# First four x tiles of a hybrid encoder step loaded as rows and turned by TensorE, before and after

## The reference, cut to what matters

```python
seq = concatenate([meta_tokens, x], axis=1)
cq, ckv_raw, kpe_raw, mq, mk, mv, mo, mi, mf, za, zb = project(rmsnorm(seq, norm_gain), w_in)   # h @ w_in
# attention from cq, ckv, kpe; mLSTM from mq, mk, mv, mo, mi, mf; gates za, zb
y = x_res + concatenate([a, m], axis=-1) @ w_out
```

## Time and profile before

| | us |
|---|---|
| median of 3 runs | 1995.39 (1994.79 to 1996.48) |
| the profiled execution | 1995.78 |
| its span, first to last instruction | 1994.0 |
| TensorE busy | 1985.5 |
| VectorE busy | 1254.3 |
| ScalarE busy | 911.5 |
| mean granted TensorE clock | 0.999 |

### The profile page before, as it was taken

One profiled execution on the slowest core, in us unless ns is written; L12 is line 12 of the kernel. 1 busy time (PEld: TensorE's weight loads), 2 busy tenths in 40 slices (PEclk: granted clock), 3 DMA queues, 4 the chain that ended last, 5 costly groups with the idle time before them and its releaser, 6 DMA issues.

```text
span 1994.0 us, 36219 instructions
## 1 busy us (share of the span) xinstructions
PE 1985.5 (100%) x14762; PEld 1961.7 (98%) x14762; DVE 1254.3 (63%) x2474; ACT 911.5 (46%) x1810; POOL 192.7 (10%) x228
## 2 busy tenths in 40 slices
PE   9999999999999999999999999999999999999998
PEld 9999999999999999999999999999999999999998
DVE  7856677677576786868777555444455664444444
ACT  5564456565444443434444444444444553333333
POOL 0011143433200000000000001000000000000000
PEclk9999999999999999999999999999999999999999
DMA  9765443333455554645545655565556556666665
GB/s 249 197 187 157 113 120 117 99 111 119 122 170 147 149 169 128 179 127 175 157 145 170 169 169 168 168 170 168 173 169 171 169 183 193 193 193 193 193 193 142
DMA packets 219262, 323.24 MB, mean 162 GB/s; under 512 B 28240, under 2 KB 100264, under 8 KB 219096
## 3 DMA queue, kind: packets, MB, share of 16 engines
q1 hardware_dynamic: 215800, 317.71, 55.3%
q10 hardware_dynamic: 3296, 3.22, 0.5%
HBM read 310.06 MB, written 9.62 MB: 160 GB/s over the span
## 4 chain that ended last, share of the span: by engine, by line
PE 99%; DVE 0%; DMA 0%; ACTq 0%; ACT 0%; issue 0%
PE bank L1884 31%; PE bank L1887 30%; PE bank L1888 30%; PE bank L2150 1%; PE bank L2120 1%; PE bank L2046 1%; PE bank L2049 1%; PE bank L2048 1%; PE bank L2222 0%; PE bank L2248 0%; PE bank L2116 0%; PE bank L2117 0%; DMA xt<-in_meta_tokens_dram 0%; PE bank L2260 0%; PE bank L2064 0%; PE bank L2065 0%
## 5 line engine op out<-in xcount | busy, mean ns | idle before, releaser
L1215 DVE TENSOR_TENSOR wlo<-raw,whi 128x512 fp32r<-128x512 f32 (+1 forms) x1256 | 811.0, 655 | 681.5 <-ACT whi L801 671.5
L1884 PE MATMUL bank<-xsplit,whi 128*128 128x288 f32 (+2 forms) x4128 | 1217.2, 295 | 2.4 <-DVE xsplit L1239 2.1
L1888 PE MATMUL bank<-xsplit,wlo 128*128 128x288 f32 (+2 forms) x4128 | 1212.1, 294 | 0.0
L1887 PE MATMUL bank<-xsplit,whi 128*128 128x288 f32 (+2 forms) x4128 | 1211.9, 294 | 0.0
L801 ACT CAST whi<-raw 128x512 fp32r<-128x512 f32 (+1 forms) x1256 | 706.8, 576 | 954.9 <-PE bank L1888 911.6
L1884 PEld LDWEIGHTS bank<-xsplit,whi 128*128 128x128 f32 (+1 forms) x4128 | 773.2, 187 | 5.1 <-issue 3.4
L1887 PEld LDWEIGHTS bank<-xsplit,whi 128*128 128x128 f32 (+1 forms) x4128 | 773.2, 187 | 2.0 <-issue 1.0
L1888 PEld LDWEIGHTS bank<-xsplit,wlo 128*128 128x128 f32 (+1 forms) x4128 | 772.8, 187 | 0.0
L1884 PE MATMUL bank<-latents,whi 128*128 128x288 f32 (+1 forms) x352 | 112.7, 320 | 0.2
L1887 PE MATMUL bank<-latents,whi 128*128 128x288 f32 (+1 forms) x352 | 106.9, 304 | 0.0
L1888 PE MATMUL bank<-latents,wlo 128*128 128x288 f32 (+1 forms) x352 | 106.7, 303 | 0.0
(11 more groups left out here) (301 smaller groups left out, 1254.8 us busy)
## 6 DMA issues: line engine op xcount, KB each, us to landing
raw<-in_w_in_dram SPq DMA_DIRECT2D x313, 512.0 KB, 3.8
raw<-in_w_out_dram SPq DMA_DIRECT2D x128, 512.0 KB, 3.8
raw<-in_w_in_dram SPq DMA_DIRECT2D x142, 256.0 KB, 3.1
raw<-in_w_q_up_dram SPq DMA_DIRECT2D x48, 384.0 KB, 3.3
raw<-in_w_kv_up_dram SPq DMA_DIRECT2D x16, 512.0 KB, 3.7
xres<-in_x_prompt_dram SPq DMA_DIRECT2D x32, 128.0 KB, 3.7
xt<-in_x_prompt_dram SPq DMA_DIRECT2D x28, 128.0 KB, 4.9
out_dram<-ytok SPq DMA_DIRECT2D x28, 128.0 KB, 3.5
```

The lines of the kernel that those rows point to most:

```text
L1215: ins = tt(lo, src, hi.bitcast(f32), ALU.subtract)
L1884: ins = mm(out, w_hi, m_hi, start=start, stop=False, **kw)
L1887: mm(out, w_hi, m_lo, start=False, stop=False, **kw)
L1888: return mm(out, w_lo, m_hi, start=False, stop=stop, **kw)
```

## The change

The first four tiles of x (512 features) are loaded with tokens in rows into a new buffer xp (96 partitions, four pieces of tokens: 96, 96, 96 and the 16 meta rows) and turned by TensorE, four transposes a tile, into banks 4 to 7. ScalarE and VectorE read them from the bank instead of from xs. To leave these banks free, the order of the first eight units is changed: k = 0 to 3 of columns 0 to 511 first (banks 0 to 3), then k = 0 to 3 of columns 512 to 1023; from unit 8 on it is as before. Tiles 0 and 1 are turned before the first matmul, tile 2 behind unit 0, tile 3 behind unit 1. The first 256 features of x are waited for before the transposes of tiles 0 and 1, the second 256 before that of tile 2. The fillers are 11, and after the transposes of tiles 0 and 1 there are eight transposes of the identity. All chunks have four tiles; chunk 0 keeps its features in natural order. xt still gets chunk 0, for the row sums, now by SP ahead of the weights of k = 13. The waits of SP's meta transfers and of ScalarE's queue for the memset are gone.

```diff
-CHUNKS = [(0, 2), (2, 2)] + [(k, 4) for k in range(4, KT, 4)]
+CHUNKS = [(k, 4) for k in range(0, KT, 4)]
+X_LED = 4
+X_TOK = [(N_META, 96), (N_META + 96, 96), (N_META + 192, 96), (0, N_META)]
-X_AHEAD = 2
-HALVES = 3
-WARM = 16
-X_PIECES = [12 if b in (0, 2, 3) else 4 for b in range(len(CHUNKS))]
-NAR_LOADS = [6, 4, 4, 4]
+HALVES = 2
+WARM = (11, 8)
+X_PIECES = [16, 12, 12] + [4] * (len(CHUNKS) - 3)
+NAR_LOADS = [4, 4, 4, 4]
...
+        def led_rows(eng, block, tiles):
+            a, z = 2 * P * block, 2 * P * block + 2 * P
+            rows, got = (x_prompt[0, 0:192, a:z], xp_in if block else x_in[0])
+            if tiles == 2:
+                eng.dma_start(xp[:, 0:2, a:z], rows.rearrange("(t p) c -> p t c", p=96)).then_inc(got, 16)
+            else:
+                eng.dma_start(xp[0:64, 2, a:z], x_prompt[0, 192:256, a:z]).then_inc(got, 16)
+        def part_of(u):
+            return (u % X_LED, u // X_LED) if u < 2 * X_LED else (u // 2, u % 2)
+        def x_after(u):
+            if u < X_LED:
+                return u
+            k = (u + 1) // 2
+            return k if u % 2 and X_LED <= k < KT else None
...
+            first_weights(0, (0,))
+            led_rows(sp, 0, 2)
+            first_weights(0, (1,))
+            led_rows(sp, 1, 2)
+            led_rows(sp, 1, 1)
+            for n in range(1, X_LED):
+                first_weights(n)
+            x_rows(sp, 1)
+            sp.wait_ge(eps_set, 4)
+            ends(1, 1)
+            first_weights(4)
+            ends(2, len(CHUNKS) - 2)
+            for k in range(5, KT):
                 if k % 4 == 3 and k < KT - 1:
                     x_rows(sp, chunk_of(k + 1))
+                if k == 13:
+                    x_rows(sp, 0)
+                    ends(0, 1)
                 first_weights(k)
...
-            x_end_rows(act, 0, 2, x_sample[0], range(4))
-            act.wait_ge(eps_set, 2)
-            x_end_rows(act, 0, 2, meta, (2, 3))
+            led_rows(act, 0, 1)
+            act.dma_start(xp[0:N_META, 3, :], meta[:, 0:X_LED * P]).then_inc(x_in[0], 16)
+            act.dma_start(xp[64:96, 2, :], x_sample[0, :, 0:X_LED * P]).then_inc(x_in[0], 16)
...
+            for u in range(2 * KT + AHEAD):            # ScalarE; VectorE in the same order
+                if u < 2 * KT:
+                    two_units(u)
+                    if x_after(u) is not None:
+                        x_tile(x_after(u))
...
+            for _ in range(WARM[0]):
                 mm(bank[3][:, 0:P], rB[:, 0:P], rB[:, 0:P], start=True, stop=True)
             pe.wait_ge(ident_in, 16)
+            def x_tile(k):
+                fill("x", 4 + k)
+                for t, (c0, n) in enumerate(X_TOK):
+                    ins = tr(bank[4 + k][:, c0:c0 + n], xp[0:n, t, k * P:k * P + P], ident[0:n, 0:n])
+                ins.then_inc(full[4 + k], 1)
+            pe.wait_ge(x_in[0], 16 * 4)
+            for k in range(2):
+                x_tile(k)
+            for _ in range(WARM[1]):
+                tr(bank[3][:, 0:P], ident, ident)
+            for u in range(2 * KT):
+                k, half = part_of(u)
+                pe.wait_ge(lo_done, u + 1)
+                if k < X_LED:
+                    pe.wait_ge(free[4 + k], use("x", 4 + k) + 1)
+                else:
+                    pe.wait_ge(xlo_d, k - X_LED + 1)
...
+                if u < 2:
+                    if u == 0:
+                        pe.wait_ge(xp_in, 16 * 2)
+                    x_tile(u + 2)
```

More of the change, by code:

```diff
@@ L96 @@
 PHASES = [
+    ("x", 1, (0, 0, 0, 0, 1, 1, 1, 1)),
     ("cq_two", 1, (1, 1, 1, 1, 1, 1, 1, 1)),
@@ L201, in gain_columns @@
     for k, m in CHUNKS:
-        t[:, G_X + k:G_X + k + m] = rows[k * P:(k + m) * P].reshape(P, m)
+        block = rows[k * P:(k + m) * P]
+        t[:, G_X + k:G_X + k + m] = block.reshape(P, m) if k else block.reshape(m, P).T
     for at, name in ((G_QR, "q_rope_norm"), (G_KR, "k_rope_norm")):
@@ L459, in w_rows @@
             k0, m = CHUNKS[chunk_of(k)]
-            return w_in[k0 * P:(k0 + m) * P, cols].rearrange("(p k) c -> p k c", k=m)[:, k - k0:k - k0 + n, :]
+            order = "(p k) c -> p k c" if k0 else "(k p) c -> p k c"
+            return w_in[k0 * P:(k0 + m) * P, cols].rearrange(order, k=m)[:, k - k0:k - k0 + n, :]
         def qk_rows(k, cols):
             k0, m = CHUNKS[chunk_of(k)]
-            rows = w_in[k0 * P:(k0 + m) * P, OFF_MQ:OFF_MV].rearrange("(p k) (s c) -> p k s c", k=m, s=2)
+            order = "(p k) (s c) -> p k s c" if k0 else "(k p) (s c) -> p k s c"
+            rows = w_in[k0 * P:(k0 + m) * P, OFF_MQ:OFF_MV].rearrange(order, k=m, s=2)
             return rows[:, k - k0, :, cols]
+        def led_rows(eng, block, tiles):
[12 more added lines that the diff above has]
+            return k if u % 2 and X_LED <= k < KT else None
         def x_rows(eng, b):
@@ L513, in group, with first_weights @@
                     between(n)
[L515 to L519, removed]
+            def first_weights(n, halves=(0, 1)):
+                s = n % RAW_SLOTS
+                if n < HALVES:
                     for half in halves:
                         sp.dma_start(raw[:, s, 512 * half:512 * half + 512],
[L522 to L539, removed]
+                                     w_rows(2 * n + half, 1, ds(OFF_CQ, 512))[:, 0, :])\
@@ new lines, in first_weights @@
+                            .then_inc(raw_in[s] if half else half_in[n], 16)
+                elif n < X_LED:
+                    sp.dma_start(raw[:, s, :].rearrange("p (k c) -> p k c", k=2),
+                                 w_rows(2 * n - X_LED, 2, ds(OFF_CQ + 512, 512))).then_inc(raw_in[s], 16)
+                else:
+                    sp.wait_ge(lo_done, 2 * n - 2 * RAW_SLOTS + 2)
+                    sp.dma_start(raw[:, s, :], w_rows(n, 1, ds(OFF_CQ, 1024))[:, 0, :]).then_inc(raw_in[s], 16)
@@ L540, in _, with ends @@
+            def ends(b, n):
                 x_end_rows(sp, b, n, x_sample[0], range(4))
                 x_end_rows(sp, b, n, meta, range(4))
-                first_weights(b + 2)
-            for k in range(6, KT):
+            first_weights(0, (0,))
[7 more added lines that the diff above has]
+            sp.wait_ge(eps_set, 4)
@@ L769, in steps @@
                 hooks(k)
[L772 to L781, removed]
         @block.scalar
@@ L814, in x_tile @@
             def x_tile(k):
-                act.wait_ge(x_turned, k + 1)
-                nc.scalar.activation(xhi[:, k, :], xs[:, k % 2, X_PAD:], ACT.Copy,
+                if k < X_LED:
+                    act.wait_ge(full[4 + k], use("x", 4 + k) + 1)
+                else:
+                    act.wait_ge(x_turned, k - X_LED + 1)
+                src = bank[4 + k][:, 0:NT] if k < X_LED else xs[:, k % 2, X_PAD:]
+                nc.scalar.activation(xhi[:, k, :], src, ACT.Copy,
                                      scale=G[:, G_X + k:G_X + k + 1]).then_inc(xhi_d, 1)
@@ L824, in cq_evict @@
                     nc.scalar.copy(cqraw[:, ds(g * 4 + ct, 1), :], bank[b0 + ct][:, 0:NQ]).then_inc(free[b0 + ct], 1)
[L826 to L831, removed]
+            for u in range(2 * KT + AHEAD):
[3 more added lines that the diff above has]
+                        x_tile(x_after(u))
+                else:
+                    cq_units(u - 2 * KT)
             cq_evict("cq_two", 0)
@@ L1238, in x_rest @@
                 dve.wait_ge(xhi_d, k + 1)
[L1239 to L1244, removed]
+                src = bank[4 + k][:, 0:NT] if k < X_LED else xs[:, k % 2, X_PAD:]
+                stt(xlo[:, k, :], src, G[:, G_X + k:G_X + k + 1], xhi[:, k, :].bitcast(f32),
+                    ALU.mult, ALU.subtract).then_inc(free[4 + k] if k < X_LED else xlo_d, 1)
             def cq_evict(phase, g, b0=0):
@@ L1250, in cq_evict @@
                         .then_inc(free[b0 + ct], 1)
[L1252 to L1267, removed]
+            for u in range(2 * KT + AHEAD):
+                if u < 2 * KT:
+                    x = x_after(u)
+                    if x is not None and x >= X_LED:
+                        x_turn(x)
+                    two_units(u)
+                    if x is not None:
+                        x_rest(x)
+                else:
+                    cq_units(u - 2 * KT)
             cq_evict("cq_two", 0)
@@ L1932, in _ @@
             pe.wait_ge(eps_set, 1)
-            for _ in range(WARM):
+            for _ in range(WARM[0]):
                 mm(bank[3][:, 0:P], rB[:, 0:P], rB[:, 0:P], start=True, stop=True)
             pe.wait_ge(ident_in, 16)
[L1936 to L1949, removed]
+            def x_tile(k):
[3 more added lines that the diff above has]
+                ins.then_inc(full[4 + k], 1)
@@ new lines, in _ @@
+            pe.wait_ge(x_in[0], 16 * 4)
[6 more added lines that the diff above has]
+                pe.wait_ge(lo_done, u + 1)
+                if k < X_LED:
+                    pe.wait_ge(free[4 + k], use("x", 4 + k) + 1)
+                else:
```

(16 more changed lines are left out.)

8 lines of the change are left out of this document (5 added, 3 removed).

## The result

The changed kernel took 1998.70 us (median of 20 runs) against 1995.53 (20 runs): ratio 1.0014, 95% interval 1.0008 to 1.0020. It is slower by 3.2 us (0.14%, clear of the noise), where 2.4 us faster were forecast, and lies outside the range. Three runs on record took far longer than all others of their kernel (2435 us here, 3991 of the kernel before, 3285 in e9) and are left out of the ratios. Its profiled execution took 1998.55 with a span of 1996.7, so 2.7 us of the loss are in the span that can be read.

The account below looks back on a forecast made before the run. TensorE, busy 1985.5 of 1994.0 us, bounds the kernel; only its opening could gain. Start 1.5 + clock 1.6 - turned tiles 0.6 = 2.5 us, taken as 2.4 for a tight tile 3: 1995.4 to 1993.0, range 1991.7 to 1995.9.

Parts of the forecast that it names:

- When x is there: Opening: last x transfer for tiles 0 and 1 issued at 2.1 us, landed at 6.1 (bounds 5.7 to 7.5).
- The chain from x: Opening, landing of x to first real matmul: transposes, ScalarE and VectorE steps; start 7.95 instead of 9.49, gain 1.5 us.
- The clock: First 16 real matmuls: pauses only 0.3 + 0.3 us, so full clock from the start, gain 1.6 us.
- A: Rival, opening: clock not up at the start or falls back once; 1994.6 or 1995.8 us; chance 0.25.
- C: Rival, opening: transfers no sooner, x at 7.5, start 9.4, clock slow; 0.5 us slower, 1995.9; chance 0.07.
- Tiles 2 and 3: Between the first units: turning them adds 2 x 0.3 = 0.6 us of TensorE (0.5 to 1.2).
- The weights of the opening: Early units, tight at unit 14 (0.5 us slack): weights issued five us sooner, 2.5 needed; cost 0, bound 2.5.
- Moved to k = 13: Chunk 0's 12 issues ahead of w13 make it 3.1 us late, 1.6 us left; cost 0, otherwise up to 3.

Follow-up runs that it names:

- e9: Kernel before with 24 fillers and the weights of k = 5 issued right behind those of k = 4: 1995.51 us, ratio 1.0002.
- e4: Changed kernel with SP issuing nothing behind the first 192 rows of x until x_chunk0's four transfers landed: 1996.45 us, one execution.
- e12: Changed kernel with 30 more identity transposes before the wait for x and no filler matmuls: one execution, first real matmul at 14.01 us.
- e3: Changed kernel without the eight identity transposes behind tiles 0 and 1: 1997.89 us, ratio 1.0013.
- e1: Changed kernel with 26 filler matmuls instead of 11: 1996.91 us, ratio 1.0007.
- e2: Changed kernel with 30 more identity transposes between the 11 fillers and the wait for x: 1996.83 us, ratio 1.0007.
- e6: Kernel before with 24 fillers instead of 16: 1995.44 us, ratio 0.9999.
- e5: Changed kernel with SP waiting for the identity table before unit 1's weights and the rest of x, 13 fillers, 6 dummies: 1996.61 us, ratio 1.0004.
- e8: Kernel before with the weights of k = 5 issued right behind those of k = 4, fillers unchanged: 1995.92 us, ratio 1.0003.

## Why the prediction was wrong, point by point

**When x is there.** This is the step that failed first. I took the time from issue to landing as 4.0 us, the value of nearly all transfers of the opening before, and 5.4 as the bound. It was 5.8, so x was there at 8.2 and not at 6.1. (The issue was 0.3 us late as well, at 2.37 instead of 2.1, since the issues on ScalarE's queue took up to 0.59 us. That e4 hit 6.1 is in part luck: this 0.3 and a landing 0.4 shorter than forecast cancel.) The rows of before were read as a latency, when they were the latency at that load: there SP was busy with the issues of x and the meta rows until 4.08 us before it came to further weights, and 0.73 MB were issued by then. The change takes that brake away: 1.2 MB are issued by 3.2 us, and by the windows the engines carried 1.6 MB before the sample rows were in. The runs part the two: 3.5 to 3.7 us with the rest held back, 5.5 to 5.8 without, and 7.1 in e12. The work whose start I counted as gained (unit 1's weights and the rest of x, issued early) was part of the load that delayed it.

**The chain from x.** Right in its length: e4 had 6.08 to 8.02, 1.94 us, where 1.8 to 1.85 were put down; ScalarE's 0.51 out of a bank was a little less than out of xs.

**The clock.** The premise was two pauses of 0.3 us. It was one of 3.1, because x was late and because the 11 fillers took 4.2 us and not 4.8. The reading that I used, that the clock fell behind a long pause, held: behind 2.1 us in the kernel before and in e3, 3.1 in the changed one. In e1, e2, e4, e6 and e9, where the pause was gone or at most 1.0 us, the clock stayed up. The doubt of the Trainium skill, page "TensorE: Matmul & The Clock Gate", section "Part 4: PE-mode transpose", that the full clock does not come on for transposes, is not borne out here: e2 kept 1.00 through 5.2 us of transposes, and in e12 they reached it.

**Rivals A and C came together.** I had priced C, x at 7.5, with the turns at full pace (start 9.4, 0.5 us slower), and A's slow turns with x at 6.1 (start 9.0). Late x makes the pause, and the pause the slow clock (e1 and e2), so the case to price was both. With the prediction's own terms that is 7.5 + 1.2 + 1.7 = 10.4, 0.9 us late, and 0.9 more for tiles 2 and 3: 1997.2, past the range and still short of 1998.7. With the measured ones it is 8.3 + 1.75 for the tiles + 1.6 for the dummies = 11.7, the measured start. The dummies that were hidden at 2.4 GHz were on the path at 1.2.

**Tiles 2 and 3.** The mechanism was right and the size was off: 0.61 us each against 0.3. The pieces were priced well (0.32), the change between kinds of work was put at nothing.

**The weights of the opening.** Cost 0 was right for what happened, since TensorE came late. For what I forecast it was short by some tenths. I had looked at one place, unit 14, with its slack of 0.5 us. Unit 10 stood beside it: in the kernel before its rest was made 0.8 us ahead of its start at 26.73 (13.21 + 104 x 0.13), and in e6 it closed first; of a lead of 1.4 us at the 97th matmul 0.5 was left at the 337th, and in e5 0.3 of 0.7. But both have the weights of k = 5 issued past 20 us. In e2, with the changed kernel's own queue, they were issued at 16.6 and landed at 23.2, and unit 10's rest was made at 24.56, 2.8 us ahead:

```profile
23.22 0.62 ACT L822 CAST whi<-raw 128x512 fp32r<-128x512 f32 x1 [0.84 <-DMA raw<-in_w_in_dram]
```

With the 97th matmul at the forecast's 21.0, unit 10 would be wanted at 24.1, so by these times some 0.4 us of the 2.4 would have gone (an estimate). What the change would bring with x at 6.1 and this queue is not shown: every run that had x so early held the queue back. The slack of the tightest later unit caps what an earlier start can bring, and should have stood in the sum.

**Moved to k = 13.** Right: no wait of TensorE stands there, and the distance from the 97th to the 337th matmul is 31.2 us in both kernels.

**What stays open.** Why the low stretch lasted 3.4 us in one kernel (and in e8) and 6.8 in the changed one and in e3; the runs show its length, not its cause. Whether x is late by the bytes or by the number of the transfers, and by those issued ahead of it alone or also by those behind it, was not parted. And no version was found that beats the kernel before beyond its interval.

## What to carry to other kernels

A landing time read from a trace belongs to the load at which it was read: when a change lets more be issued sooner, price what will be under way, not only the number of issues in front. In a kernel whose main engine never stops, ask for each later unit how much ahead its operands are, in the issue order that the change makes; while that order stays, an earlier start brings little more than the smallest of these. And when one lateness causes another (late data, a pause, a lower clock), price the rivals together.

## What the runs showed of the hardware that was not expected

The fillers' pace is not the same from one execution to the next: 11 of them took 4.21 us in the changed kernel and 4.90 in e3, and the step to full pace came at about 4.4 us there and at about 6.8 in e1. A tile of four transposes (304 columns) between matmuls cost 0.61 us at 2.4 GHz where its pieces cost 0.32. The same issue order gave landings of the same 64 KB between 5.5 and 7.1 us. And 3.4 us at half the clock take 0.0009 off the mean of an execution, so those of the kernel before whose mean is 1.000 did not have them; their median spans (1993.65, 1993.8 and 1993.45 us on three chips) are at most 0.35 us under those with 0.999 (1993.85, 1993.85, 1993.8). As in e6, the slow stretch of that kernel's opening costs little at the end.
